# A hybrid decoder layer on 8 cores: an earlier gate for the first weights, spare products, a spread-out memory norm, and a last norm shared by three engines

## The reference, cut to what matters

```python
h = x
h = h + 0.5 * swiglu(rmsnorm(h, ffn1_norm), ffn1_wg, ffn1_wu, ffn1_wd)     # D_FF = 2816
u = rmsnorm(h, mix_norm)
z = u @ w_in                                                                # all branch inputs and gates
merged = g0 * mla(z) @ mla_w_o + g1 * gla(z) @ gla_w_o + g2 * cross(z, rmsnorm(mem, mem_norm)) @ x_w_o
h = h + merged @ w_out
h = h + 0.5 * swiglu(rmsnorm(h, ffn2_norm), ffn2_wg, ffn2_wu, ffn2_wd)
return rmsnorm(h, final_norm)
# rmsnorm(x, g) = x * rsqrt(mean(x*x) + 1e-6) * g,   mem is 256 x 1024 for each sequence
```

## Time and profile before

| | |
|---|---|
| median of three runs | 1629.36 us (1628.25, 1629.36, 1754.62) |
| the profiled execution | 1627.07 us |
| its span, slowest core (core 2) | 1626.0 us |
| spans of the cores | 1618.5 to 1626.0 us |
| PE busy | 1588.4 us, 98% of the span |
| DVE, ACT, POOL busy | 884.8, 738.6 and 120.9 us |
| HBM | 283.16 MB read, 54.26 MB written |

### The profile page before, as it was taken

The page is one execution under the profiler, slowest core; times in us unless marked ns, Lnnn a source line. Parts: engine busy times, 40 slices in busy tenths (PEclk is TensorE's granted clock), DMA queues, the critical chain, the costliest instruction groups (busy, mean ns, idle before and its releaser), DMA issues.

```text
span 1626.0 us, 23823 instructions; the slowest of 8 cores (1618.5 to 1626.0 us)
## 1 busy us (share of the span) xinstructions
PE 1588.4 (98%) x7517; PEld 737.7 (45%) x7667; DVE 884.8 (54%) x1524; ACT 738.6 (45%) x1193; POOL 120.9 (7%) x227
## 2 busy tenths in 40 slices
PE   6999999999999999999999999999999999999997
PEld 2444444444444444444444444444444444444444
DVE  6666333557766466664565454476444445533347
ACT  5212211046765237882276874258587632311114
POOL 1101111100000000000000000000000000001000
PEclk9999999999999999999999999999999999999999
DMA  8779999997767455586787788587334344522212
GB/s 209 115 113 130 133 127 143 123 180 187 166 108 179 153 162 147 99 199 198 237 227 165 180 204 220 184 278 232 104 96 125 115 158 160 177 85 91 78 52 104
DMA packets 80712, 249.65 MB, mean 154 GB/s; under 512 B 9488, under 2 KB 13840, under 8 KB 80144
## 3 DMA queue, kind: packets, MB, share of 16 engines
q0 software_dynamic: 28720, 107.43, 38.3%
q1 hardware_dynamic: 51872, 140.70, 26.9%
HBM read 283.16 MB, written 54.26 MB: 208 GB/s over the span
## 4 chain that ended last, share of the span: by engine, by line
PE 94%; DMA 2%; DVE 1%; issue 1%; ACT 1%; POOL 0%; SPq 0%; DVEq 0%; ACTq 0%; POOLq 0%
PE ps_all L561 94%; DMA ring<-f1g 1%; DMA ring<-wb 1%; DVE hS L599 1%; DMA hS<-x 0%; ACT L587 0%; DVE mb L599 0%; ACT mb L587 0%; ACT ma L587 0%; DVE ntm L599 0%; PE ps_all L572 0%; DVE ma L594 0%; ACT fa L587 0%; DVE mb L611 0%; POOL ring L206 0%
## 5 line engine op out<-in xcount | busy, mean ns | idle before, releaser
L561 PE MATMUL ps_all<-ntm,ring 128*128 128x512 bf16 x2181 | 529.1, 379 | 3.6 <-ACT mb L587 0.6
L561 PE MATMUL ps_all<-B,ring 128*128 128x512 bf16 x1971 | 448.4, 379 | 2.7 <-DVE mb L594 0.2
L561 PEld LDWEIGHTS ps_all<-ntm,ring 128*128 128x128 bf16 x2224 | 217.1, 98 | 257.2 <-issue 4.3
L561 PEld LDWEIGHTS ps_all<-B,ring 128*128 128x128 bf16 x2016 | 196.6, 98 | 233.1 <-issue 1.1
L561 PE MATMUL ps_all<-aF,ring 128*128 128x512 bf16 (+1 forms) x1240 | 294.8, 374 | 4.9 <-DVE mb L599 3.1
L587 ACT ACTIVATE fa<-ps_all 128x512 f32<-128x512 f32 x170 | 101.3, 597 | 364.1 <-PE ps_all L561 351.8
L599 DVE SCALAR_TENSOR_TENSOR hS<-ps_all,hS 128x512 f32<-128x512 f32 (+1 forms) x256 | 170.1, 672 | 86.5 <-PE ps_all L561 85.4
L594 DVE TENSOR_TENSOR aF<-fa,ps_all 128x512 bf16<-128x512 f32 x151 | 103.2, 686 | 196.3 <-PE ps_all L561 186.1
L587 ACT ACTIVATE mb<-ps_all 128x512 bf16<-128x512 f32 (+1 forms) x304 | 165.5, 572 | 72.7 <-PE ps_all L561 70.6
L561 PEld LDWEIGHTS ps_all<-aF,ring 128*128 128x128 bf16 x1264 | 123.4, 98 | 143.6 <-issue 6.7
L587 ACT ACTIVATE ma<-ps_all,hv 128x512 f32<-128x512 f32 x104 | 71.1, 686 | 173.0 <-PE ps_all L561 164.9
(11 more groups left out here) (139 smaller groups left out, 1193.8 us busy)
## 6 DMA issues: line engine op xcount, KB each, us to landing
ring<-wb SPq DMA_DIRECT2D x112, 512.0 KB, 4.7
ring<-f1g POOLq DMA_DIRECT2D x44, 512.0 KB, 8.5
ring<-f2bg POOLq DMA_DIRECT2D x44, 512.0 KB, 3.9
wb<-wm POOLq DMA_DIRECT2D x28, 512.0 KB, 13.8
ma<-spill SPq DMA_DIRECT2D x48, 256.0 KB, 4.8
ring<-wb SPq DMA_DIRECT2D x48, 256.0 KB, 3.8
ring<-f2g POOLq DMA_DIRECT2D x22, 512.0 KB, 7.8
f2bg<-ring SPq DMA_DIRECT2D x22, 512.0 KB, 6.9
```

The lines of the kernel that those rows point to most:

```text
L561: i = e.matmul(_ap(o), lhsT=_ap(l), rhs=_ap(r), start=st, stop=sp)
```

## The change

There are five edits. `vecs` is loaded behind the first quarter of tile 0 instead of behind all four. `first[0]` depends on `x0[0]` instead of `x0[1]`. For tile 0 in the opening, products on `ones` whose result nobody reads are put behind the squares' products: one each for chunks 1 to 6, six for chunk 7, into a bank of their own. The memory norm's 8 products get the priority `LATER // 2` and a recorded duration of 1.2 instead of 0.4. In the last step, chunks 2 and 6 of each half are multiplied by the root on POOL (`tensor_tensor`) and then by the vector on ACT (Copy with a scale), instead of both in one DVE instruction.

```diff
@@ load_x
             ops.append(op)
+            if t == 0 and c == 0:
+                f.dma("sp", vecs, vecs_d, nbytes=128 * NV * 4)
         return ops
 
     x0 = load_x(0, 0)
-    f.dma("sp", vecs, vecs_d, nbytes=128 * NV * 4)
@@ memory_kv
-        rmsnorm(src, [vcol(V_MEM + c) for c in range(8)], D, dst, NMEM, "n")
-        M2.put(*memf)
+        p = mean_square(src, D, NMEM, "n", M2, M1)
+        rstd = M2.get()
+        power(rstd[:, 0:NMEM], p[:, 0:NMEM], -0.5, EPS)
+        f.base = LATER // 2
+        for c in range(8):
+            f.add([("dve", lambda e, c=c: e.scalar_tensor_tensor(
+                out=_ap(dst[c]), in0=_ap(src[c]), scalar=_ap(vcol(V_MEM + c)), in1=_ap(rstd[:, 0:NMEM]),
+                op0=ALU.mult, op1=ALU.mult), 1.2)], outs=[dst[c]], ins=[src[c], vcol(V_MEM + c), rstd])
+        f.base = 0
+        M2.put(rstd, *memf)
@@ open
         p = bank("n")
+        idle = bank("n") if t == 0 else None
         for c in range(8):
             ts(raw_at[t][c], hslot[t][c], vcol(V_F1 + c), None, ALU.mult)
             sq = M1.get()
             actf(sq, hslot[t][c], AF.Square, scale=D ** -0.5)
             mm([(p, ones, sq, c == 0, c == 7)])
+            for _ in range(0 if t else 6 if c == 7 else 1 if c else 0):
+                mm([(idle, ones, sq, True, True)])
             M1.put(sq)
@@ the gates of the opening
-    first[0].deps.add(x0[1].seq)
+    first[0].deps.add(x0[0].seq)
@@ ending
             for c in range(8):
-                scaled(hh[h][c], hh[h][c], V_FIN, c, r[:, 0:256])
+                if c in (2, 6):
+                    f.add([("pool", lambda e, o=hh[h][c], r=r[:, 0:256]: e.tensor_tensor(
+                        out=_ap(o), in0=_ap(o), in1=_ap(r), op=ALU.mult), 0.8)], outs=[hh[h][c]], ins=[hh[h][c], r])
+                    actf(hh[h][c], hh[h][c], AF.Copy, scale=vcol(V_FIN + c))
+                else:
+                    scaled(hh[h][c], hh[h][c], V_FIN, c, r[:, 0:256])
```

## The result

The changed kernel takes 1635.57 us in the median of 6 runs (1634.35 to 1641.98). Against runs of the kernel before on the same chip its ratio is 1.0054, with a 95% interval of 1.0040 to 1.0067, or 6.5 to 10.9 us of 1627. Ratios and profiles here are of executions in which no die (cores 0 to 3, 4 to 7) ran longer at a lower granted clock than the other. I had predicted 1627.1 with a range up to 1631: the time is above the range and the direction was wrong. The profiled execution took 1641.98 us. It is the slowest of the six, so its holes are larger than those of a median execution.

A forecast was written before the change was run, and what follows sets the result against it. PE, busy 98% of the span, was taken as the bound, leaving its ends, holes and low-clock products. Gate -0.7, spare products 0, norm 0 and tail -1.6 took 1629.36 to 1627.1; own range 1625.5 to 1629.0, with rivals 1622 to 1631.

The forecast's parts named there:

- The step that failed: Memory norm: its eight reordered products stay hidden by full banks or the late f1d load, worth 0.
- Rival D: ffn1a: later key products hold ring buffers longer, making one new hole of 4.8 us, time 1631.9; chance 12%.
- seven buffers: ffn1a: the argument, without a size, against late key products holding up the weight loads in the ring.
- The reading of the hole at 166 us: PE's 3.10 us hole before 168.94 on core 2 is a late f1d load, not the norm's burst.
- Rival C: Hole at 166 us is the norm's burst; removing it gains 3.1 us plus 1.7 of low clock, median 1622.7; 17%.
- The gate: Opening: first weight loads issued 1.8 us sooner, worth -0.7 us, ends 0 and -1.8.
- Rival E: Opening gives nothing, as DMAs are full and spare products delay the first real ones; 1627.8, no chance of its own.
- The spare products: Opening: twelve unread products keep PE busy before the first eight real ones; worth 0 on core 2.
- The tail: Last step: four of DVE's 16 products go through POOL and ACT; -1.6 us, ends -1.6 and +1.2.
- Rival B: Last step: POOL and DVE take turns, so the tail grows by 1.2 us, time 1629.9; chance 22%.
- DVE is the bound of this tail: End of the kernel: DVE's 16 products, 0.40 us each, 6.41 us in all, set the tail.
- The sum: Whole kernel, core 2: -0.7, 0, 0 and -1.6 make -2.3 us, span 1623.7, median 1627.1.

The follow-up runs named there:

- norm_only: The kernel before with the memory norm's edit alone (priority LATER // 2, recorded duration 1.2); ratio 1.0031, 5.0 us slower.
- f1d_first: The kernel before with one f1d load moved ahead of two wb conversions on POOL's queue, the norm's burst unchanged; ratio 1.0000.
- tail_split: The kernel before with the first of the four last output DMAs cut into two of two chunks each; ratio 1.0002.
- tail_pairs: The kernel before with the last outputs in eight transfers of two chunks (256 KB) instead of four of four; ratio 0.9991.
- tail_ps: The kernel before with the last step's edit alone, but the root that DVE reads put in PSUM; ratio 1.0008.
- tail_both: tail_pairs with chunks 2 and 6 of the second half alone on POOL and ACT, and DVE's root in PSUM; ratio 1.0004.
- tail_fine: tail_pairs with each of the last two chunks sent by itself (128 KB); ratio 0.9998.

## Why the prediction was wrong, step by step

**The step that failed** is "Nothing is added but order: the same 8 products at 0.41 us. They are hidden [...] so I take 0." The eight products were indeed hidden; what waits for them was not. I priced the order of the DVE products and not the order of what reads them, nor that of POOL's queue, which the plan changed with it. The key and value products moved by some 22 us; they had given the next load its time to land, and they hold weights in the ring. I took 0, and norm_only measured +5.0 us. Rival D named this mechanism and the side on which it falls, at 12%, and its price of 4.8 us for one hole is near the 5.0 us of norm_only. That nearness is luck, since the loss came as several smaller holes. What I set against it, "seven buffers", is where it went wrong. The row that decides was at hand: DMA was full from 160 to 360 us (share 0.99 on core 1). The 40 us with idle DMA were not made up by 320 us, for all seven buffers; I had read the DMA share in the opening alone. D was too cheap in one more way: it came at 184, at 328 and at 370 us, not once.

**The reading of the hole at 166 us** was right: the named releaser was not the cause, the late f1d load was the earlier trace rows (f1d_first). Rival C's 3.1 us and clock gain were not to be had even so, since without the hole the time stays.

**The gate** (I took -0.7): the issue at 7.67 and the third load's 1.0 us gain on core 2 came as told, and so did its danger, that x0's second half is in flight. The size was wrong as a whole: all cores together it gives 0.10%, 1.6 us, on the other side, if it is anything (the interval touches 1). I followed core 2, a late core, and not the four cores that began at 14.4. Those got later. That the path to the end isn't set by one core's opening is my reading, not shown. Rival E (opening worth nothing) was nearer.

**The spare products** (I took 0): 1.0002, right for them alone. The low level vanishes in the first eight products, and the third group starts no sooner. I had allowed them up to 0.7 us in front of weights that land early. Beside the sooner gate they can cost over 3, since they wait for tile 0's last quarter and the weights don't.

**The tail** (I took -1.6, with +1.2 as the other end): by the trace it is +0.8. Rival B is shown. Four DVE products are stretched from starts 0.40 apart to 0.79 to 0.87, +1.8 us, and four fewer save 1.6: DVE ends at +5.88 and not +5.67. The last output is issued at +6.01 for +5.75 and takes 3.3 for 3.0, which makes 0.6 of the 0.8. The other 0.2 is SP: on all eight cores the span ends 0.23 us behind the last landing, before 0.03, as four of its last semaphore waits, 0.05 us each, now stand behind it. The Trainium skill's "SBUF — State Buffer", section "SBUF: two separate sides", was the only source that spoke against this part. By that rule, the traces agree: DVE products with two SBUF inputs go from 0.47 to 0.94 us beside POOL's, and stay at 0.47 with one input in PSUM. They don't block in full, by the rule read strictly: each POOL product adds about 0.45 us to DVE, where POOL alone takes 0.72. The Trainium skill's "GPSIMD Engine Reference", section "Performance versus the Vector engine", gave me an estimate of 0.6 to 0.7 us for POOL's product; its 2.6 cycles at 1.2 GHz alone make an estimate of 0.55 for 256 elements. The undisturbed ones took 0.71 to 0.73.

"DVE is the bound of this tail" fits the kernel before, where an earlier first output (tail_split) changes nothing, but moving products off DVE isn't the way to use it. What could be had cheaply was the landing behind it, 0.4 to 0.8 us by smaller outputs (tail_pairs), the one variant here whose interval lies at or below 1.

**The sum.** In place of -0.7, 0, 0 and -1.6 the parts measured +1.6 (gate), +0.3 (spare products), +5.0 (norm) and +0.8 (tail, by the trace), which makes 7.7 of the 8.8 us. The single small ones are each hardly larger than their intervals. (The low end of the forecast's own range, 1625.5, doesn't come out of its terms either: 1629.36 - 1.8 - 1.6 is 1626.0.)

**What stays open**: which of the three things behind the late keys and values costs how much; a run with the late products and the two conversions back in their place would tell. That DMA moves fewer bytes in the slow kernels while it is as busy is mostly the mix of its queues. By the page of the kernel after, POOL's queue took 38.8% for 107.43 MB and SP's 27.8% for 140.70 MB. So a byte costs 1.8 times as much on POOL's queue, counted as written; its loads read f32 and write bf16, so by bytes read it is 0.9 times. From 200 to 360 us SP's part fell from 4.15 to 1.01 MB, and POOL's rose from 18.06 to 18.90. Open too is how the gate's 0.10% comes to the end of the slowest core.

## What to carry to other kernels

When operations are only reordered, follow what reads their results and which buffers those readers free, and look at the DMA share of the next few hundred us: where it is full, a load delayed once can be paid for again at later waits. Look also at what stands behind a load that is blocked on its queue: conversions that need no buffer waited there while DMA was idle. A knob that is harmless alone may not be so with another (the rank and the cost here), so what the planner makes of both is to be read as an order of instructions, not as an intention. A load issued sooner among full DMAs can land when it did before, or later; and at the end of this kernel the size of the last transfer was worth more than sharing out the arithmetic.

## What the runs showed of the hardware

- A DVE product of 128x256 f32 lasts 0.47 us, with both tiles in SBUF or one of them in PSUM. Starts are 0.40 apart; where DVE waits on its own semaphore for the product just before, they are 0.59 apart (tail_ps, tail_both). So a wait on the instruction just ahead costs 0.19 us, on one engine.
- POOL's product of 128x256 f32 takes 0.71 to 0.73 us beside DVE products with one PSUM input, and up to 1.00 beside those with two SBUF inputs, which it stretches from 0.47 to 0.94.
- The last output from SBUF lands 3.0 us behind its issue with 512 KB (before), 2.2 to 2.6 with 256 KB (tail_pairs) and 1.9 to 2.6 with 128 KB (tail_fine), where the end came no sooner. With 512 KB issued 1.0 us behind one another it is up to 4.4 (tail_ps).
- A converting load of 512 KB on POOL's queue took 8.7 to 9.3 us in the opening of the kernel before, 13.6 at 164 us, 23.4 at 290 us, and 33.5 at 299 us of the kernel after, each with DMA full or nearly so.
